# A hybrid decoder layer on one Trainium2 core: every second weight unit of five stick-breaking projections as seven block products in place of eight

## What is computed

```
h = rms_norm(x, norm_mix[l])
proj = h @ w_in[l]                     # 2048 x (512 + 256 + 64 + 3 * 1024)
c_q, c_kv, k_pe, q_sb, k_sb, v_sb = jnp.split(proj, IN_SPLITS, axis=-1)
...
o_sb = stick_breaking_attention(q_sb, k_sb, v_sb)
x = x + mixed @ w_out[l]
x = x + memory_cross_attention(...)
x = x + hierarchical_moe(...)          # 32 experts, all weights are read
```

## Time and profile before

| | us |
|---|---|
| median of 3 runs | 1352.51 (1351.83 to 1352.7) |
| the profiled execution, its own time | 1350.58 |
| its span, first to last instruction | 1348.8 |
| TensorE busy over the span | 992.5 (74%) |
| VectorE, ScalarE, GpSimd busy | 576.0, 303.9, 40.9 |
| DMA | 486.40 MB, 361 GB/s on average |

### The profile page before, as it was taken

How to read it: one execution, slowest core, us unless ns; L and a number is a source line. 1 busy time by engine, 2 the same in 40 slices (tenths; PEclk the granted TensorE clock), 3 DMA queues, 4 the chain that set the end, 5 groups by cost and what they waited for, 6 DMA issues and landing times.

```text
span 1348.8 us, 20643 instructions
## 1 busy us (share of the span) xinstructions
PE 992.5 (74%) x8516; PEld 595.7 (44%) x8516; DVE 576.0 (43%) x1132; ACT 303.9 (23%) x537; POOL 40.9 (3%) x92
## 2 busy tenths in 40 slices
PE   8999999999999975666555666655566655566656
PEld 7888898888888522222222222212222222222222
DVE  5555567776656643233322233332223332223324
ACT  5554457774544100000000000000000000000002
POOL 1300000130000000000000000000000000000001
PEclk9999999999999997778777778787787787777878
DMA  7777764447869999999999999999999999999997
GB/s 245 262 243 250 214 176 125 152 150 276 290 235 354 359 432 429 434 431 432 430 432 434 430 430 430 434 431 430 430 435 431 431 431 431 434 431 430 430 427 307
DMA packets 78021, 486.40 MB, mean 361 GB/s; under 512 B 9944, under 2 KB 25438, under 8 KB 64799
## 3 DMA queue, kind: packets, MB, share of 16 engines
q1 hardware_dynamic: 77484, 483.46, 89.0%
q10 hardware_dynamic: 306, 2.11, 0.4%
q0 software_dynamic: 192, 0.31, 0.2%
HBM read 481.14 MB, written 4.72 MB: 360 GB/s over the span
## 4 chain that ended last, share of the span: by engine, by line
PE 50%; DMA 46%; SPq 1%; DVE 1%; issue 1%; ACT 0%; DVEq 0%; ACTq 0%
DMA gu<-in_w_up 42%; PE ps L1053 10%; PE ps L606 8%; PE ps L608 8%; PE ps L607 8%; PE ps L1108 5%; DMA down<-in_w_down 4%; PE ps L1032 2%; PE ps L1065 1%; PE ps L586 1%; PE ps L851 1%; PE ps L852 1%; PE ps L853 1%; PE ps L778 1%; SPq L471 0%
## 5 line engine op out<-in xcount | busy, mean ns | idle before, releaser
L1053 PE MATMUL ps<-gu,xe 128*32 128x256 f32 x3968 | 284.9, 450 | 305.8 <-DMA gu<-in_w_up 305.3
L2144 DVE TENSOR_TENSOR x_sum<-ps,x_sum 128x512 f32<-128x512 f32 x240 | 149.1, 684 | 508.3 <-PE ps L1065 508.3
L1053 PEld LDWEIGHTS ps<-gu,xe 128*32 128x32 f32 x3968 | 139.7, 129 | 468.9 <-DMA gu<-in_w_up 328.5
L1619 DVE TENSOR_TENSOR w_lo<-w_raw,w_hi 128x1024 fp32r<-128x1024 f32 (+1 forms) x137 | 164.6, 1207 | 117.7 <-ACT w_hi L1226 114.2
L606 PE MATMUL ps<-w_hi,a_hi 128*128 128x512 f32 (+1 forms) x468 | 183.3, 392 | 0.0
L607 PE MATMUL ps<-w_lo,a_hi 128*128 128x512 f32 (+1 forms) x468 | 179.8, 384 | 0.0
L608 PE MATMUL ps<-w_hi,a_lo 128*128 128x512 f32 (+1 forms) x460 | 176.8, 384 | 0.0
L1226 ACT ACTIVATE w_hi<-w_raw 128x1024 fp32r<-128x1024 f32 (+1 forms) x137 | 141.9, 1040 | 128.7 <-PE ps L608 98.2
L1538 ACT ACTIVATE sg<-ps 128x128 f32<-128x128 f32 x31 | 8.6, 278 | 654.3 <-PE ps L1053 654.3
L1108 PE MATMUL ps<-down,act_t 128*32 128x512 f32 x976 | 112.4, 601 | 6.1 <-DMA down<-in_w_down 6.1
L607 PEld LDWEIGHTS ps<-w_lo,a_hi 128*128 128x128 f32 x468 | 88.0, 188 | 16.4
(11 more groups left out here) (335 smaller groups left out, 831.6 us busy)
## 6 DMA issues: line engine op xcount, KB each, us to landing
down<-in_w_down SPq DMA_DIRECT2D x29, 4096.0 KB, 22.7
gu<-in_w_gate SPq DMA_DIRECT2D x28, 4096.0 KB, 31.7
gu<-in_w_up SPq DMA_DIRECT2D x28, 4096.0 KB, 40.9
w_raw<-in_w_in SPq DMA_DIRECT2D x56, 512.0 KB, 5.1
w_raw<-in_w_out SPq DMA_DIRECT2D x32, 512.0 KB, 4.4
gu<-in_w_up SPq DMA_DIRECT2D x18, 512.0 KB, 6.1
w_raw<-in_w_mem_kv SPq DMA_DIRECT2D x16, 512.0 KB, 3.5
down<-in_w_down SPq DMA_DIRECT2D x13, 512.0 KB, 15.2
```

The lines of the kernel that those rows point to most:

```text
L1053: mm = pe.matmul(ps[5][j * SLOTS:(j + 1) * SLOTS, 0:2 * P].rearrange("s (m f) -> s m f", m=2), xe[:, k, :], gu[side][:, :, k, j * P:(j + 1 ...
L1619: ve.tensor_tensor(w_lo[:, u % RING, :, 0:n], w_raw[:, u % RING, :, 0:n], w_hi[:, u % RING, :, 0:n], ALU.subtract).then_inc(S("w_split"), 1)
L2144: ins = ve.tensor_tensor(x_sum[:, t, cols], ps[g][:, :], (x_res if first else x_sum)[:, t, cols], ALU.add)
```

## The change

In the five chunks `SEVENS` (`SB_Q`, `SB_Q + 1`, `SB_K`, `SB_K + 1`, `SB_V`) the 8 units are taken as four pairs `m`. The second unit of a pair is done as before. The first is a product of a 2 x 2 block matrix of tokens (2 token halves x 2 k-tiles) with a 2 x 2 block matrix of weights (2 k-tiles x 2 halves of 256 columns): eight block products of 12 matmuls in all before, now seven of three matmuls of 256 columns each, into four PSUM banks in place of two. Three products use weights as they are (or one block of them), four use sums.

- Sums of tokens (`s_raw`, `s_hi`, `s_lo`), once for all chunks: `sum_rows` on VectorE, rounded by ScalarE, split by VectorE.
- Sums of weights (`t_raw`), once a pair: `sum_weights` on GpSimd (one instruction of 512 elements a partition, two of 256), then rounded by ScalarE into `t_hi` and split by VectorE into `t_lo`. `t` has two buffers; `t_lo` lies in the place of `t_raw`. GpSimd's sums of pair `m` wait for the products of pair `m - 2` (`t_used`). The slot of a first unit comes free for its next load only when it has been summed too.
- The first unit is rounded and split without its first 256 columns (768 elements in place of 1024).
- Sums of outputs: `sum_sevens` on VectorE, nine instructions of 256 columns a chunk, into `seven_sum` in SBUF, from where ScalarE copies on. TensorE waits for the sums of the chunk before last, whose banks it takes.
- The load of `mem_sb` moves from the end of `KV_LAT` to after `SB_V`; `move_quads` stands two loads later; the transposes of the latents stand inside a chunk; some semaphores are merged.

```diff
+SEVENS = [SB_Q, SB_Q + 1, SB_K, SB_K + 1, SB_V]
+PAIRS = KD // UK // 2
+SEVEN_PAIRS = PAIRS * len(SEVENS)
...
+        t_hi = place("t_hi", [P, 2, 4 * HN], F32R, offset=v_mla_at)
+        t_raw = place("t_raw", [P, 2, 4 * HN], offset=km_at)
+        t_lo = place("t_lo", [P, 2, 4 * HN], F32R, offset=km_at)
+        seven_sum = place("seven_sum", [P, TT, UN], offset=qpe_at)
+        seven_part = place("seven_part", [P, 3, HN], offset=e_at + 85 * 1024 + 512)
...
                     sp.wait_ge(S("w_split"), u - RING + 1)
+                    if seven_first(u - RING):
+                        sp.wait_ge(S("t_summed"), seven_of(u - RING) + 1)
...
+            def triple(dst, xh, xl, wh, wl, start=False, stop=False):
+
+                pe.matmul(dst, xh, wh, start=start, stop=False)
+                pe.matmul(dst, xh, wl, start=False, stop=False)
+                return pe.matmul(dst, xl, wh, start=False, stop=stop)
...
+            def project_sevens(c, between):
+
+                b = acc_bank(c)
+                left, right = slice(0, HN), slice(HN, UN)
+                rows = [slice(t * P, (t + 1) * P) for t in range(TT)]
+                for m in range(PAIRS):
+                    i, n = 2 * m, PAIRS * SEVENS.index(c) + m
+                    u, first, last = POS[(c, i)], m == 0, m == PAIRS - 1
+                    wh, wl = w_hi[:, u % RING], w_lo[:, u % RING]
+                    a11h, a11l = a_hi[:, UK * i, rows[0]], a_lo[:, UK * i, rows[0]]
+                    a12h, a12l = a_hi[:, UK * i + 1, rows[0]], a_lo[:, UK * i + 1, rows[0]]
+                    a22h, a22l = a_hi[:, UK * i + 1, rows[1]], a_lo[:, UK * i + 1, rows[1]]
+                    pe.wait_ge(S("w_rounded"), u + 1)
+                    pe.wait_ge(S("w_split"), u + 1)
+                    triple(ps[b + 2][:, left], a11h, a11l, wh[:, 0, right], wl[:, 0, right], start=first)
+                    triple(ps[b][:, right], a12h, a12l, wh[:, 1, right], wl[:, 1, right], start=first)
+                    triple(ps[b][:, left], s_hi[:, m, 3], s_lo[:, m, 3], wh[:, 1, left], wl[:, 1, left]
+                           ).then_inc(S("w_used"), 1)
+                    if m in between:
+                        between[m]()
+                    u += 1
+                    pe.wait_ge(S("w_rounded"), u + 1)
+                    pe.wait_ge(S("w_split"), u + 1)
+                    for j in range(UK):
+                        k = (i + 1) * UK + j
+                        for t in range(TT):
+                            mm = triple(ps[b + t][:, :], a_hi[:, k, rows[t]], a_lo[:, k, rows[t]],
+                                        w_hi[:, u % RING, j, :], w_lo[:, u % RING, j, :],
+                                        start=first and t == 1 and j == 0,
+                                        stop=last and t == 0 and j == UK - 1)
+                    mm.then_inc(S("w_used"), 1)
+                    pe.wait_ge(S("t_rounded"), n + 2)
+                    pe.wait_ge(S("t_split"), n + 3)
+                    th, tl = t_hi[:, n % 2], t_lo[:, n % 2]
+                    for g, (dst, xh, xl) in enumerate((
+                            (ps[b + 2][:, right], s_hi[:, m, 0], s_lo[:, m, 0]),
+                            (ps[b + 3][:, right], s_hi[:, m, 2], s_lo[:, m, 2]),
+                            (ps[b + 3][:, left], s_hi[:, m, 1], s_lo[:, m, 1]),
+                            (ps[b + 1][:, right], a22h, a22l))):
+                        cols = slice(g * HN, (g + 1) * HN)
+                        mm = triple(dst, xh, xl, th[:, cols], tl[:, cols], start=first and g == 1,
+                                    stop=last and g != 1)
+                    mm.then_inc(S("t_used"), 1)
...
+                if c == SB_Q:
+                    pe.wait_ge(S("split_lo"), KD)
+                    pe.wait_ge(S("t_rounded"), 1)
+                    pe.wait_ge(S("t_split"), 2)
+                elif c == SB_Q + 1:
+                    pe.wait_ge(*chunk_out(KV_LAT))
+                elif c in SEVENS:
+                    pe.wait_ge(S("seven_summed"), SEVENS.index(c) - 1)
...
+                if c in SEVENS:
+                    project_sevens(c, {2: turn_q} if c == SB_K else {2: turn_kv} if c == SB_K + 1 else {})
+                else:
+                    project(c)
+            pe.wait_ge(S("seven_summed"), len(SEVENS))
...
+                    if seven_first(u):
+                        sc.activation(plain_cols(w_hi, u), plain_cols(w_raw, u), ACT.Copy).then_inc(
+                            S("w_rounded"), 1)
+                        continue
                     sc.activation(w_hi[:, u % RING, :, 0:n], w_raw[:, u % RING, :, 0:n],
                                   ACT.Copy).then_inc(S("w_rounded"), 1)
+                    m = seven_of(u)
+                    if m is not None:
+                        sc.wait_ge(S("t_summed"), m + 1)
+                        if m >= 2:
+                            sc.wait_ge(S("t_used"), m - 1)
+                        sc.activation(t_hi[:, m % 2, :], t_raw[:, m % 2, :], ACT.Copy).then_inc(
+                            S("t_rounded"), 1)
                 done[0] = max(done[0], upto)
...
+                if c == SB_K:
+                    rounded(START[c] + 5 + RING)
+                    split_head("q", 48, hi=cq_hi)
+                if c == SB_K + 1:
+                    rounded(START[c] + 5 + RING)
+                    split_head("kv", 52, hi=ckv_hi)
+                rounded(DONE[c] + RING + (1 if c in SEVENS else 0))
                 if c == Q_LAT:
                     chunk_copy(c, lambda t: c_q[:, t, :], SS_X)
+                    sc.wait_ge(S("t_split"), 1)
+                    sc.activation(s_hi[:, :, :, :].rearrange("p m s q -> p (m s q)"),
+                                  s_raw[:, :, :, :].rearrange("p m s q -> p (m s q)"), ACT.Copy).then_inc(
+                                      S("t_rounded"), 1)
...
+                    if seven_first(u):
+                        ve.tensor_tensor(plain_cols(w_lo, u), plain_cols(w_raw, u), plain_cols(w_hi, u),
+                                         ALU.subtract).then_inc(S("w_split"), 1)
+                        continue
                     ve.tensor_tensor(w_lo[:, u % RING, :, 0:n], w_raw[:, u % RING, :, 0:n],
                                      w_hi[:, u % RING, :, 0:n], ALU.subtract).then_inc(
                                          S("w_split"), 1)
+                    m = seven_of(u)
+                    if m is not None:
+                        ve.wait_ge(S("t_rounded"), m + 2)
+                        ve.tensor_tensor(t_lo[:, m % 2, :], t_raw[:, m % 2, :], t_hi[:, m % 2, :],
+                                         ALU.subtract).then_inc(S("t_split"), 1)
...
+            def sum_rows():
+
+                def rows(t, k):
+                    return s_sum[:, :, k, t * P:(t + 1) * P]
+
+                ve.wait_ge(S("split_lo"), KD)
+                even = [a.rearrange("p (i j) q -> p i (j q)", j=2 * UK)[:, :, 0:UK * SEQ]
+                        for a in (a_hi[:, :, :], a_lo[:, :, :])]
+                link(ve.tensor_tensor(s_sum[:, :, :, :].rearrange("p i j q -> p i (j q)"), even[0], even[1],
+                                      ALU.add))
+                link(ve.tensor_tensor(s_raw[:, :, 0], rows(1, 0), rows(1, 1), ALU.add))
+                ve.tensor_tensor(s_raw[:, :, 2], rows(0, 0), rows(1, 0), ALU.subtract)
+                link(ve.tensor_tensor(s_raw[:, :, 1], s_raw[:, :, 0], rows(0, 0), ALU.subtract))
+                ve.tensor_tensor(s_raw[:, :, 3], rows(0, 1), s_raw[:, :, 1], ALU.subtract).then_inc(
+                    S("t_split"), 1)
+
+            def sum_sevens(c):
+
+                n, b = SEVENS.index(c), acc_bank(c)
+                left, right = slice(0, HN), slice(HN, UN)
+                part = [seven_part[:, g, :] for g in range(3)]
+                p1, p5, p6, p7 = (ps[b + 2 + g][:, half] for g in range(2) for half in (left, right))
+                ve.wait_ge(S("t_used"), PAIRS * (n + 1))
+                if n >= 1:
+                    ve.wait_ge(*chunk_out(SEVENS[n - 1]))
+                link(ve.tensor_copy(part[0], p1))
+                ve.tensor_tensor(part[1], p6, part[0], ALU.add)
+                link(ve.tensor_tensor(seven_sum[:, 0, right], ps[b][:, right], part[0], ALU.add))
+                ve.tensor_tensor(part[0], p5, part[1], ALU.add)
+                link(ve.tensor_tensor(part[2], p7, part[1], ALU.add))
+                ve.tensor_tensor(seven_sum[:, 0, left], ps[b][:, left], part[0], ALU.add)
+                ve.tensor_tensor(seven_sum[:, 1, right], ps[b + 1][:, right], part[2], ALU.add)
+                link(ve.tensor_tensor(part[1], p5, part[2], ALU.add))
+                ve.tensor_tensor(seven_sum[:, 1, left], ps[b + 1][:, left], part[1], ALU.add).then_inc(
+                    S("seven_summed"), 1)
+
+            sum_rows()
...
+                if c == SB_K:
+                    split_w(START[c] + 5 + RING)
+                    split_rest("q", 48, hi=cq_hi, lo=cq_lo)
```

(35 more changed lines are left out.)

83 lines of the change are left out of this document (48 added, 35 removed).

## The result

The changed kernel takes 1392.43 us (1391.37 to 1396.57, 4 runs) against 1352.58 (1351.83 to 1352.7): a ratio of 1.0302, 95% interval 1.028 to 1.0323. The direction was right, the size was not: 39.9 us slower, where the sum said 19.5, and 6.4 us above the range.

What follows compares the result with a forecast made beforehand. TensorE was taken to bound the changed first stage, DMA the experts. 1350.6 - 4.7 (TensorE) + 5.6 (`KV_LAT`) + 8.5 (chunk changes) + 10 (GpSimd against VectorE) = 1370.0, as a median 1372 us; range 1358 to 1386.

Steps and rivals of the forecast that it cites:

- The wait in `KV_LAT`: Before unit 12 in `KV_LAT`, TensorE waits for VectorE's split, delayed by token sums and angles: +5.6 us (5 to 6).
- Nothing behind it gives the time back: After `KV_LAT`: its +5.6 us wait is not recovered later, since TensorE is the bound.
- TensorE's gain: Twenty pairs in the five chunks: 5.20 us each in place of 5.44, giving -4.7 us.
- GpSimd against VectorE: Five chunks: GpSimd's sums and VectorE's splits contend, and `c_q` scaling delays sums: +10 us (0 to 22).
- They nearly take turns: Earlier trace, split at 294.35 beside a GpSimd sum: 0.83 us lost over 1.31 us of overlap.
- The move: SyncE's queue, chunk's move two loads later: loads behind it still fit; 0, at most 1 us a chunk.
- I take 0, at most 1 a chunk: Cost in us given to the chunk's move holding SyncE's queue, with following loads issued about 22 us after chunk start.
- Changes of chunk: Sums, rounding and splits delay TensorE: 1.4 us each in `SB_K`, `SB_K + 1`, `SB_V`, 4.2 in `SB_Q + 1`; +8.5 (4 to 12).
- its slack hides the last sums: After `SB_V`, the next chunk is a plain one whose slack covers the last output sums, so no cost.
- Without contention: Rival for the whole kernel: only chains in order count, +9.4 us, 1362 median; chance 0.27 shared with half made good.
- Carried one to one: Time won or lost before the experts moves their start and reaches the kernel's end in full.
- GpSimd is the bound: Rival in the five chunks: GpSimd's sums stretch beyond 5.2 us a pair; 1383 to 1387; chance 0.14 (above 1380).

Runs made afterwards that it cites:

- e1: Changed kernel with VectorE's splits of units 12 to 15 in `KV_LAT` moved ahead of the split of the token sums and the angles; 1392.37 us.
- e14: Changed kernel with only `KV_LAT` reordered: angles and sums of rows between VectorE's splits, Sin earlier; 1379.97 us.
- e8: e7 with GpSimd's three sums of weights a pair replaced by a memset, so its result lacks them; 1348.64 us.
- e2: Changed kernel with GpSimd's three sums of weights a pair replaced by one memset, all waits kept; 1376.18 us.
- e7: Changed kernel with third weight-sum buffer, `KV_LAT` reordered, scaling of `c_q` and `c_kv` within chunks, move's fetch three loads behind its store; 1366.78 us.
- e15: e7 with GpSimd's operations, sized like the sums, on its own tile; nobody waits for them, zeros are split instead; 1360.16 us.
- e16: Kernel before the change, with GpSimd's three operations a pair, sized like the sums, running beside it on its own tile; 1351.34 us.
- e13: Changed kernel with only the move split: fetch of its quads three loads behind its store; 1383.4 us.
- e11: e7 with store and fetch of a move together again, as in the changed kernel; 1380.94 us.
- e10: e7 with the three sums of weights a pair made by VectorE and none by GpSimd; 1366.28 us.
- e6: Changed kernel with a third buffer for the sums of weights, VectorE's order unchanged; 1388.89 us.
- e12: e7 with GpSimd's norms and scaling of `c_q` and `c_kv` back between the chunks; 1363.83 us.
- e5: Changed kernel with matmuls of no use filling TensorE's waits, half as many as in e4; 1393.63 us.
- e4: Changed kernel with filler matmuls of 128 columns ahead of nine TensorE waits, all work and waits kept; 1398.93 us.

## Why the prediction was wrong

- **The wait in `KV_LAT`, right.** +5.6 predicted, 5.45 measured, at the place and by the releaser named. VectorE's `s_sum` took 2.29 and each `s_raw` 0.69, and the split that TensorE wanted began at 45.18, within 1.2 us of the working. "Nothing behind it gives the time back" was too simple: e1 removed the wait and gained nothing, e14 rearranged the same work with the Sin and gained 12.5. The step priced the wait and not the lead of VectorE and ScalarE that the later chunks live on.
- **TensorE's gain, right.** Pairs take 5.23 us where 5.20 was predicted, 4.2 us for twenty in place of 4.7; e8 keeps 3.6 of it in the stage.
- **GpSimd against VectorE, the right mechanism, under-sized.** +10 predicted in a range of 0 to 22; e2 gives 16.2 and e8 to e7 18.1. "They nearly take turns" was the reading of the earlier trace rows (it left out GpSimd's next sum, at 295.80, which meets the same split for another 0.27 us), and then the middle was taken because GpSimd runs free in the output sums. The Trainium skill's sentence on shared SBUF interfaces (GPSIMD Engine Reference, "Key points") is borne out by e15 and e16: 1.43 us for a split that takes 1.22 alone. The condition for a cost is missing from sentence and step alike: VectorE must have little idle time left. The step's own account of a chunk ran from 22.2 to 25.5 us; the five chunks of e7 take 24.4 each on average, in its upper half.
- **The move, the step that failed.** "I take 0, at most 1 a chunk" was the text; the edit that undoes it is worth 9.0 us in the changed kernel (e13) and 14.2 in e7's order (e11). The working let the loads behind the move be issued 22 us after a chunk's start. In the trace the store itself is at 98.37, 22.4 us into `SB_Q + 1`, and the next load at 105.42, 29.5 us in. The store was not waiting for its data: the copy was done at 92.69, and in the next three chunks 2.6 to 3.0 us before the store. It stood in the queue behind a weight load, issued at 97.96 when the split at 96.71 freed its slot, and that split had waited for the copy and the table loads on ScalarE. The hold behind it was in the earlier trace rows, 8.3 us long. It was priced on a clean schedule, while the other waits had already used the lead that was to hide it.
- **Changes of chunk, under-sized.** Waits of over 0.3 us against the working: in `SB_Q + 1` 2.75 for the scaling of `c_q` (3 predicted), then 1.24 and 4.45 before and in the third pair (4.2 predicted); in `SB_K` 3.2, in `SB_K + 1` 4.0 and in `SB_V` 4.6, where 1.4 each stood; in `SB_V + 1` 2.9, where "its slack hides the last sums" stood. The text had the places right, and its sizes fit up to the first move. Without the hold (e13) 3.2 stay in each of the three and none in `SB_V + 1`.
- **Without contention, under-sized as a whole.** The prediction had +9.4 over before; e2, which has no sums, is +24.5. The missing 15.1 us are order: e7's order takes 27.5 from e2. Each part was in the text, but added as a separate small term where each made the next one's cover smaller. In e8 the changes of chunk cost 1.1 us (142.4 against 146.0 - 4.7) where 8.5 stood; but e8 also has the third buffer and GpSimd's 0.95 us memset for 3.8 us of sums, so this is not their cost in the changed kernel.
- **Carried one to one, right:** 42.1 in the stage, 39.9 in the medians.
- **The rival "GpSimd is the bound"**, 1383 to 1387, came nearest in time and was wrong in cause: GpSimd is busy 89 of 160 us, and e10, where it makes no sums, is no faster than e7.

The miss of 20.4 us is thus some 15 of order and some 6 of contention (together 0.9 too much, because the kernel before ran 0.9 us faster beside e2 than in the result). How the 15 divide is less certain: the edits by themselves give 9.0 (e13), 12.5 (e14) and 3.5 (e6), 25.0 in all, together 28.6 (e12), and they include what the prediction had priced (5.6 in `KV_LAT`, 4.2 for the table loads).

## What to carry to other kernels

Before work is moved to helpers, add up each helper's busy time over a whole chunk, with the slowdown that they do to each other, and compare it with the bound's: slowed instructions cost nothing on an engine that is half idle (e16) and about half of their excess on one that is nearly full (e15: 11.5 of 23.5 us). When an engine loses its lead, price what was hidden behind that lead again, a held queue above all, and not one term after another on a schedule that stays clean. Slow matmuls behind a wait are not yet a loss that can be won back; fill the wait and look whether the time moves (e5).

## What the runs showed of the hardware that was not expected

- After a wait of 4.45 us TensorE's matmuls of 512 columns start 0.43 us apart for 2.6 us, at a granted clock of 0.50, and then 0.23 again. Stretches behind waits of 5.45 and 2.75 us show a granted clock of 0.78 and 0.77 (46.15 to 55.00, 82.66 to 90.00). The Trainium skill (TensorE: Matmul & The Clock Gate, "Part 1") says that the array's clock is 1.2 GHz when it idles; the trace agrees, and e5 adds that with the clock at 0.99 the kernel was no faster.
- A matmul of fp32 operands and 128 columns is two instructions and takes 0.223 us (e4), 1.9 times what the filler was sized by.
- A VectorE split of two SBUF operands goes from 1.22 to 1.43 us in the mean beside GpSimd, the split of `t_lo` from 1.25 to 1.77 (e8, e15), and GpSimd's 512-element operation, 1.27 at its shortest in the changed kernel, takes 1.52 to 1.78 in the mean (e15, e7). It makes little difference whether the operands are the same tiles (1.40 in e7) or others (1.43 in e15, 1.44 in e16).
- SyncE's queue held for 8 us by a store's wait costs nothing in the kernel before, where TensorE never waits in the five chunks. Held for 7 to 10 us it costs 9.0 us in the changed kernel (e13) and 14.2 in e7's order (e11), with the same instructions in it.
